# Moving 106 of 281 low-part subtractions from VectorE to GpSimd in a two-block transformer kernel

## The reference

```python
def swiglu(u, wg, wu, wd):
    return (jax.nn.silu(u @ wg) * (u @ wu)) @ wd
...
# first block, layer i: m is silu(c) @ ada_w[i] + ada_b[i], cut in 9 parts
x = x + 0.5 * m[:, 2] * swiglu(modulate(x, norm_g[i, 0], m[:, 0], m[:, 1]), ...)
x = x + m[:, 5] * mixer(...)        # layer 0: a two-way state-space scan (SSD), layer 1: pooling
x = x + 0.5 * m[:, 8] * swiglu(modulate(x, norm_g[i, 2], m[:, 6], m[:, 7]), ...)
# second block: projections (w_in_2), gated recurrence and sparse attention, w_out_2, twice
```

## Time and profile before

| | before |
|---|---|
| median of 3 runs | 2466.79 us (2463.68 to 2474.09) |
| the profiled execution | 2466.79 us, span 2465.1 us |
| PE busy | 2231.3 us (91%) |
| DVE busy | 1611.7 us (65%) |
| ACT busy | 988.4 us (40%) |
| POOL busy | 182.5 us (7%) |
| chain that ended last | PE 71%, DVE 18%, issue 6%, ACT 5% |
| low parts on VectorE, line 1631 | 281, 641.0 us |

### The profile page before, as it was taken

The page is one execution under the profiler, slowest core; times in us unless marked ns, Lnnn a source line. Parts: engine busy times, 40 slices in busy tenths (PEclk is TensorE's granted clock), DMA queues, the critical chain, the costliest instruction groups (busy, mean ns, idle before and its releaser), DMA issues.

```text
span 2465.1 us, 39886 instructions
## 1 busy us (share of the span) xinstructions
PE 2231.3 (91%) x16565; PEld 2132.5 (87%) x16565; DVE 1611.7 (65%) x2268; ACT 988.4 (40%) x1109; POOL 182.5 (7%) x152
## 2 busy tenths in 40 slices
PE   7888889988998988999899899979999999899987
PEld 6888888888985988898899899979999788799967
DVE  6877767778878976777754654456763445675453
ACT  2422254434332554332433443445444435544432
POOL 1000000000001000001000000002310000321000
PEclk7888999998998889999999999989998798899779
DMA  8565757753322426777555445534333133434301
GB/s 295 178 221 202 256 182 256 261 179 104 103 79 100 139 95 228 234 255 241 184 180 181 134 137 189 185 103 150 125 122 112 43 120 104 136 122 120 103 18 52
DMA packets 270792, 383.83 MB, mean 156 GB/s; under 512 B 8441, under 2 KB 230727, under 8 KB 270679
## 3 DMA queue, kind: packets, MB, share of 16 engines
q1 hardware_dynamic: 246983, 293.59, 36.3%
q0 software_dynamic: 22288, 85.02, 10.3%
q10 hardware_dynamic: 1408, 3.59, 0.4%
HBM read 381.06 MB, written 1.11 MB: 155 GB/s over the span
## 4 chain that ended last, share of the span: by engine, by line
PE 71%; DVE 18%; issue 6%; ACT 5%; SPq 0%; DMA 0%; DVEq 0%; ACTq 0%
PE bank L615 20%; PE bank L616 19%; PE bank L617 19%; DVE ada_acc L1677 4%; ACT w_hi L1209 3%; DVE w_lo L1631 3%; PE bank L991 2%; PE bank L628 2%; PE bank L650 1%; DVE e_long L1954 1%; DVE e_long L1972 1%; DVE rstd L1641 1%; DVE conv_acc L1903 1%; PE bank L637 1%; DVE e_short L1957 1%
## 5 line engine op out<-in xcount | busy, mean ns | idle before, releaser
L1631 DVE TENSOR_TENSOR w_lo<-raw,w_hi 128x2048 fp32r<-128x2048 f32 (+1 forms) x281 | 641.0, 2284 | 503.9 <-ACT w_hi L1209 503.6
L615 PE MATMUL bank<-u_hi,w_hi 128*128 128x256 f32 x2376 | 703.5, 296 | 26.4 <-DVE u_lo L1662 24.1
L616 PE MATMUL bank<-u_lo,w_hi 128*128 128x256 f32 x2376 | 689.4, 290 | 0.0
L617 PE MATMUL bank<-u_hi,w_lo 128*128 128x256 f32 x2376 | 688.6, 290 | 0.0
L1209 ACT ACTIVATE w_hi<-raw 128x2048 fp32r<-128x2048 f32 (+1 forms) x281 | 531.5, 1893 | 234.1 <-PE bank L617 220.3
L615 PEld LDWEIGHTS bank<-u_hi,w_hi 128*128 128x128 f32 x2376 | 472.6, 199 | 43.0 <-issue 35.0
L616 PEld LDWEIGHTS bank<-u_lo,w_hi 128*128 128x128 f32 x2376 | 474.3, 200 | 0.5 <-issue 0.5
L617 PEld LDWEIGHTS bank<-u_hi,w_lo 128*128 128x128 f32 x2376 | 473.6, 199 | 0.0
L1677 DVE SCALAR_TENSOR_TENSOR ada_acc<-ada,silu_c,ada_acc 128x256 f32<-128x256 f32 x588 | 266.5, 482 | 13.0
L615 PE MATMUL bank<-h_hi,w_hi 128*128 128x256 f32 x880 | 248.1, 282 | 20.6 <-DVE h_lo L1705 20.6
L616 PE MATMUL bank<-h_lo,w_hi 128*128 128x256 f32 x880 | 247.3, 281 | 0.0
(11 more groups left out here) (334 smaller groups left out, 3769.0 us busy)
## 6 DMA issues: line engine op xcount, KB each, us to landing
ada<-in_ada_w POOLq DMA_DIRECT2D x72, 1024.0 KB, 5.8
raw<-in_w_in SPq DMA_DIRECT2D x60, 1024.0 KB, 5.0
raw<-in_ffn_w_gate SPq DMA_DIRECT2D x55, 1024.0 KB, 7.0
raw<-in_ffn_w_up SPq DMA_DIRECT2D x55, 1024.0 KB, 5.1
raw<-in_ffn_w_down SPq DMA_DIRECT2D x55, 1024.0 KB, 5.1
raw<-in_ssd_w_in SPq DMA_DIRECT2D x20, 1024.0 KB, 5.3
raw<-in_w_out SPq DMA_DIRECT2D x16, 1024.0 KB, 5.1
raw<-in_ssd_w_out SPq DMA_DIRECT2D x8, 1024.0 KB, 5.2
```

The lines of the kernel that those rows point to most:

```text
L615: pe.matmul(out_, wh, xh, start=start, stop=False, skip_group_check=True)
L616: pe.matmul(out_, wh, xl, start=False, stop=False, skip_group_check=True)
L617: return pe.matmul(out_, wl, xh, start=False, stop=stop, skip_group_check=True)
L1631: ve.tensor_tensor(wlo[slot][:, 0:n], raw[slot][:, 0:n], whi[slot][:, 0:n].bitcast(F32), ALU.subtract)\
```

## The change

GpSimd takes over 106 of the 281 low parts: in every feed-forward the down chunks but the last (10 in each), in `ffn0` to `ffn2` also the gate chunks from block 2 on (`GATES_BY_POOL`, 9 in each), in `ffn0` also the up chunks from block 1 on (`UPS_BY_POOL`, 10), and in the state-space stage chunks 3 to 15 and 17 to 22 (19). VectorE's queue loses the same instructions. On GpSimd's queue they stand between the `ada` loads: low part of up, low part of gate, load for q+2, low part of down, load for q+3. In the state-space stage twelve stand ahead of the store of `q`, one behind the first skip product and six behind the broadcast loads of `q`. The instruction, its operands and the semaphores are the same; the engine differs.

```diff
+GATES_BY_POOL = (0, 1, 2)
+UPS_BY_POOL = (0,)
...
@@ gpsimd, in ffn(i, loads)
-                def pair(j, layer):
+                def lo(r, j):
+
+                    slot = (g + r) % SLOTS
+                    pool.wait_ge(S["hi_done"], g + r + 3 * j + 1)
+                    pool.tensor_tensor(wlo[slot][:, :], raw[slot][:, :], whi[slot][:, :].bitcast(F32), ALU.subtract)\
+                        .then_inc(lo_done[slot], 1)
+
+                def pair(j, layer, more=True, first=False):
+                    if not first and i in UPS_BY_POOL:
+                        lo(1, j)
+                    if more and not first and i in GATES_BY_POOL:
+                        lo(2, j)
                     if layer is not None:
                         load_on(0, j, layer)
+                    if more:
+                        lo(3, j)
+                    if layer is not None:
                         load_on(1, j, layer)
...
-                        pair(j0, layer)
+                        pair(j0, layer, j0 < FP - 1, j0 == 0)
...
-            ffn(0, [(1, FP - 1, 0), (FP - 1, FP, 0)])
+            ffn(0, [(0, 1, None), (1, FP - 1, 0), (FP - 1, FP, 0)])
...
@@ gpsimd, state-space stage
+            for c in range(G["ssd_in"] + 3, G["ssd_in"] + 15):
+                lo(c)
...
+                if t == 0 and h0 == 0:
+                    lo(G["ssd_in"] + 15)
...
+                if gd >= 2:
+                    lo(G["ssd_in"] + 15 + gd)
...
-            ffn(3, [(1, LAST_PAIRS, 1)])
+            ffn(3, [(0, 1, None), (1, LAST_PAIRS, 1), (LAST_PAIRS, FP - 1, None)])
+            ffn(4, [(0, 1, None), (1, FP - 1, None)])
...
@@ vector, in ffn(i)
-                    lo(g + 4, CH, j - 1)
+                    if i not in UPS_BY_POOL:
+                        lo(g + 4, CH, j - 1)
                     if vectors:
                         sum_of(q, 0, half_q, vectors)
-                    if not last:
+                    if not last and i not in GATES_BY_POOL:
                         lo(g + 5, CH, j - 1)
-                        lo(g + 6, CH, j - 1)
...
-                lo_at(g + 3)
...
@@ vector, state-space stage
-            lo_at(c0 + 3)
...
-                lo_at(c0 + 4 + i)
...
-                if 1 <= gd < 7:
-                    lo_at(c0 + 16 + gd)
```

More of the change, by code:

```diff
@@ L508, in ffn @@
             def ffn(i, loads):
+                g = G[FFNS[i][0]]
                 q0 = ADA_FIRST + ADA_FFN * i - 2
@@ L531, in _ @@
                 load_ada(q, q % 2, 0)
-            ffn(0, [(1, FP - 1, 0), (FP - 1, FP, 0)])
+            ffn(0, [(0, 1, None), (1, FP - 1, 0), (FP - 1, FP, 0)])
             second = (ADA_CHUNKS - ADA_FIRST - ADA_FFN) // 2
-            ffn(1, [(1, second, 0), (second, FP - 1, 1)])
+            ffn(1, [(0, 1, None), (1, second, 0), (second, FP - 1, 1)])
             pool.wait_ge(S["mods_done"], ADA_FIRST + 2 * ADA_FFN)
@@ L546, in _, with lo @@
                 pool.memset(cpad[i][:, :, :, :], 0.0).then_inc(S["set_up"], 1)
+            def lo(c):
+                slot = c % SLOTS
+                pool.wait_ge(S["hi_done"], c + 1)
+                pool.tensor_tensor(wlo[slot][:, :], raw[slot][:, :], whi[slot][:, :].bitcast(F32), ALU.subtract)\
+                    .then_inc(lo_done[slot], 1)
+            for c in range(G["ssd_in"] + 3, G["ssd_in"] + 15):
+                lo(c)
             pool.wait_ge(S["dt_cols"], 1)
@@ L581, in _ @@
                 .then_inc(S["pool_in"], 16)
-            ffn(2, [(1, FP - 1, 1), (FP - 1, FP, 1)])
-            ffn(3, [(1, LAST_PAIRS, 1)])
+            ffn(2, [(0, 1, None), (1, FP - 1, 1), (FP - 1, FP, 1)])
+            ffn(3, [(0, 1, None), (1, LAST_PAIRS, 1), (LAST_PAIRS, FP - 1, None)])
+            ffn(4, [(0, 1, None), (1, FP - 1, None)])
             for l in range(DEPTH):
```

## The result

The changed kernel takes 2600.99 us (median of 4 runs, 2595.12 to 2607.05), the kernel before in the same runs 2467.61 us. The ratio is 1.0535 (95% interval 1.051 to 1.0562). The forecast was slower, at 2509 us and at most 2592 us: the direction came true, the size did not.

The account below looks back on a forecast made before the run. TensorE was taken to set the end, with VectorE ahead of it in places. Terms of 21.4 + 6.3 + 3.5 + 6.5 + 4.1 = 42 us on 2466.79 gave 2509 us; 8-in-10 range 2435 to 2592 us.

Parts of the forecast that it names:

- the stall is not paid: Rival: in the 27 modulation pairs GpSimd's reads slip between VectorE's chained steps; 2379 us, chance 0.25.
- the price of one moved low part: Where VectorE always has two-input work: 3.8 us on GpSimd, stalling VectorE's queue by 3.3 us.
- B: Stall on VectorE's own queue for each low part moved to GpSimd: 3.3 us, likeliest 3.1 to 3.5.
- the price is higher: Rival: 2048 elements cost by slower GpSimd rows, stall 4.3 us or more; 2585 us; chance 0.18 together with the clock rival.
- Pairs of `ffn1` and `ffn2`: 18 one-vector pairs, gate and down moved: 21.47 us against 20.28, +1.19 us each, +21.4 us.
- Pairs of `ffn0`: All three low parts moved: six two-vector pairs +6.3 us, three one-vector pairs +3.5 us.
- State-space stage: Six scan low parts +6.5 us, four early convolution ones +4.1 us, the other moved ones zero.
- as long as B is under 4.0 us: Later state-space convolutions: VectorE's 1.75 us wait for ScalarE hides the 1.03 us loss, zero below that stall.
- +1.03 each: First four convolution low parts, VectorE back to back: stall replaces a 2.27 us low part, +4.1 us together.
- The scan's term: Six scan low parts amid gapless two-input VectorE work: +(3.3 - 2.21) x 6 = +6.5 us.
- `ffn3` and `ffn4`, GpSimd's queue, the loads: 20 down low parts covered by TensorE's 12 us; loads and stores delayed behind low parts still timely: all zero.
- TensorE's clock: Rival: added TensorE waits lower its clock, 2.2 us in each of 27 pairs; 2569 us; chance 0.18 together with higher price.

Follow-up runs that it names:

- write-only kernel: Changed kernel with state-space low parts back on VectorE and GpSimd's feed-forward low parts replaced by a one-column subtraction and two memsets: 2388.34 us, ratio 0.9683.
- experiment 4: Changed kernel with all 106 GpSimd low parts reading `raw` twice, 3.60 us in place of 4.56, `w_lo` zero: 2512.17 us, ratio 1.0166.
- experiment 6: Changed kernel with both `ada` loads of a pair issued behind the down low part on GpSimd: 2681.8 us, ratio 1.0857.

## Why the prediction was right and wrong

**Right: the mechanism.** VectorE and GpSimd keep each other out of SBUF, whole instructions at a time, as the earlier trace rows had it. The write-only kernel shows that neither GpSimd's writes nor its busy time hold up the chained steps. The Trainium skill (SBUF — State Buffer, section Who interferes with whom) says that a VectorE instruction with two SBUF inputs contends with a GpSimd instruction that reads SBUF, and not with one that only writes it. The stalls of 4.20 us and the steps of 482 ns beside memsets agree. What the forecast did not have is that "turns" are not strict: in the scan one of GpSimd's low parts stood behind nearly 8 us of VectorE's instructions, and in the write-only kernel a VectorE step stood behind two memsets. The rival "the stall is not paid" is out. Its price was a fair one: 2401 us without the state-space gain, and the write-only kernel takes 2388.

**Wrong: the step "the price of one moved low part".** It took 3.8 us for the instruction and 3.3 us for B, and held to the level differences "because they have the same two plain inputs". They don't: one is a broadcast, and so is one input of the multiplication in the earlier trace rows from which the 3.1 us came. The instruction takes 4.56 us and B is 4.20 and 5.03 us in a pair of `ffn1`, 4.6 us on average. How much each place lost follows. The rival "the price is higher" (B of 4.3 or more, 2585 us and above) is what happened, and the figure of the Trainium skill that the forecast set aside, by which the sum would have been near 2590 us, was the better one.

**Pairs of `ffn1` and `ffn2`: forecast +21.4, measured +54.1 us.** With 9.23 us for the two stalls in place of 6.6 the term is 24.10 - 20.28 = 3.8 us, times 18, or 69 us. That is too much by 15, from a second slip in the same step: 20.28 us was the length of the fastest pairs. The six pairs of `ffn1` from 398.19 to 524.19 in the earlier trace rows are 126.00 us, 21.0 each, because two of them ran at a lower clock. From 21.0 the sum is 3.1 x 18 = 56 us, within 2 us of the measurement. With this base and the forecast's B it would have been +8 us. So it is partly luck that the short version of experiment 4, whose low parts are about as long as the forecast had them, lands at 2512 us beside the forecast 2509. Its `ffn0` is +10.4 us (forecast 9.8), its `ffn1` +8.1 (10.7), its state-space stage +16.0 (10.6).

**Pairs of `ffn0`: forecast +9.8, measured +32.4.** The three pairs with one vector went from 62.0 to 74.2 us, +12.2, forecast +3.5. The six with two vectors went from 149.9 to 172.8 us, +22.9, forecast +6.3. They were to take 16.32 + 3B, with the measured stalls over 29 us. The first takes 32.6 us, the others 28.0 on average. The timeline of one of 27.6 us shows why:

```profile
156.90 5.62 DVE L1709 SCALAR_TENSOR_TENSOR ada_acc<-ada,silu_c,ada_acc 128x256 f32<-128x256 f32 x14
166.64 0.17 DVE L1719 TENSOR_TENSOR mods<-bank,cols 128x8 f32 x1 [4.12 <-PE bank L682]
...
142.86 9.35 POOL L525 TENSOR_TENSOR w_lo<-raw,w_hi 128x2048 fp32r<-128x2048 f32 x2 [3.13 <-ACT w_hi L1241]
...
158.04 8.92 POOL L525 TENSOR_TENSOR w_lo<-raw,w_hi 128x2048 fp32r<-128x2048 f32 x1
```

Up and gate low part stretch sum q from 6.15 to 14.6 us (141.87 to 156.46), by 8.4. The down low part comes at 158.04, in sum q+1, whose steps keep their usual 5.62 us; it is GpSimd that waits, until VectorE is done at 162.52, and it ends 4.4 us later. VectorE is not stalled a third time. But its wait for `ada_sums` of q+1, which TensorE comes to only behind the up chunk, holds it 4.12 us, and from the end of the sum to the end of `h_lo` it is 6.77 us in place of 4.02. 16.32 + 8.4 + 2.75 = 27.5 us. So here it is two stalls and a wait for TensorE, where the forecast had three stalls.

**State-space stage: forecast +10.6, measured +34.7.** By the starts of the `conv`s, it divides as follows. Up to the first one, the low part in the dt chain: +0.4, forecast zero. From the first to the fifth: 33.34 to 46.32 us, +13.0, forecast +4.1. From the fifth to the twelfth: 90.59 to 99.19 us, +8.6, forecast zero "as long as B is under 4.0 us". From there to VectorE's first wait for `cb` in the scan: 52.51 to 56.52 us, +4.0, forecast zero. The scan with its six low parts (777.39 to 884.39 before, 863.35 to 976.24 after): 107.00 to 112.89 us, +5.9, forecast +6.5. The rest: +2.9, forecast zero.

In the first four of the convolution, the step "+1.03 each" set a stall against the low part that went and forgot that this low part had filled a time in which VectorE would else wait for ScalarE. For the later ones B is above the 4.0 us that was named as the end of the cover, but only by 0.2 us each, and they lost 1.2 on average. VectorE still waits 0.8 to 3.6 us for `conv_pad` in each of the last ones, so ScalarE runs later too: its own wait for `conv_acc` went from 39.6 to 73.4 us. Which of ScalarE's operations makes it late was not followed up.

The scan's term came out nearly as forecast, but not by its working. VectorE waits there 2.13 us for `cb` in every second step, and every second low part gets in during that wait:

```profile
886.64 2.54 DVE L2001 SCALAR_TENSOR_TENSOR e_long<-e_long,tok_cols,cb 128x256 f32<-128x256 f32 x1 [2.13 <-ACT cb L1445]
...
890.43 4.72 DVE L2003 SCALAR_TENSOR_TENSOR e_short<-e_short,tok_cols,cb 128x128 f32<-128x128 f32 x1
```

Three low parts stall VectorE 2.1 us (2.54 in place of 0.48), the three that follow them 4.2 to 4.4 us (4.72 in place of 0.34). That is 19.2 us, less six times 2.21, or 6.0 us: a B of 3.2 us on average, from another cause than the forecast's 3.3.

**`ffn3` and `ffn4`, GpSimd's queue, the loads: forecast nothing, and nearly nothing it was.** `ffn4` has -0.4 us, and the write-only kernel, with the same queue, lost nothing. `ffn3` has +2.5 us, and about as much in every kernel with full low parts there (210.2 to 211.6 us against 208.5).

**The second block, +9.7 us, with no changed line.** In the other kernels' profiles the same code takes 843.8 to 853.6 us, against 843.8 in the profile of before. It is thus within the spread of single profiles, from the low end of it to the high. The rival "TensorE's clock" is seen only in part: `ffn1` went from 0.96 to 0.93, `ffn2` from 0.94 to 0.89, and TensorE's busy time in `ffn2` from 215.78 to 228.11 us. It comes with the waits, and no run takes the two apart.

## What to carry to other kernels

Before work moves to an idle engine, price the moved instruction by a row with the same operand forms (dense, broadcast, one tensor or two), and ask for how long it will keep the other engine out of memory; here 2.2 us of VectorE became 4.2 to 5.0 us of VectorE. If the reason for the move is a wait in an in-order queue, try first to put other ready work ahead of the waiting instruction: that alone gave 3.7%, with nothing moved. And place a stall by who is behind it: with the same two low parts a pair took 24.1 us when they were spread and 27.6 when they stood together ahead of TensorE's reduction.

## What the runs showed of the hardware

- GpSimd's `tensor_tensor` of 128x2048: 4.56 us with two different dense inputs, 3.60 us with a broadcast input or the same tensor twice, 4.70 us with float32 in place of fp32r output; 2.39 us for 1024.
- A memset of 128x3072 (2.66 us) or 128x2047 (1.81 us) on GpSimd stalls no VectorE step with two wide inputs: the slowest of 588 is 490 ns. It does stall a TENSOR_SCALAR of 128x256 with one wide input: 27 of 84 took over 0.6 us, up to 4.63, in place of 0.35.
- Low parts keep that TENSOR_SCALAR out as well: 3.69 us in place of 0.35. It is a short form, 0.35 us where a SCALAR_TENSOR_TENSOR of the same size takes 0.48; whether all one-input instructions behave so no run shows.
- The waiting goes the other way too. In the scan one of GpSimd's low parts took 12.23 us:

```profile
916.56 0.34 DVE L1986 SCALAR_TENSOR_TENSOR e_short<-q_bcast,tok_cols,consts 128x128 f32<-128x128 f32 x1
919.03 2.61 DVE L2001 SCALAR_TENSOR_TENSOR e_long<-e_long,tok_cols,cb 128x256 f32<-128x256 f32 x1 [2.13 <-ACT cb L1445]
...
909.13 12.23 POOL L569 TENSOR_TENSOR w_lo<-raw,w_hi 128x2048 fp32r<-128x2048 f32 x1 [4.58 <-ACT w_hi L1241]
```

It ended at 921.36, 4.46 us after VectorE's first gap began at 916.90; until then VectorE ran unhindered. In the pair of `ffn1` shown, where each step of `ada_acc` waits for the one before, GpSimd's low part of 458.45 keeps out the step that starts 0.27 us later. With two vectors a step waits only for the one before of its own vector, so the steps follow each other more closely (14 in 5.62 us against 7 in 3.61). There it got in at once at 142.86 and only at the end of the sum at 158.04. What decides it is open.
- The down low part in `ffn1` starts right behind the issue of an `ada` load (0.90 us), and VectorE's stall is 5.03 us, 0.8 us more than without one. In the changed kernel 21 low parts right behind an issue stall a step of `ada_acc` by 4.74 to 5.20 us, and each of these steps had started 0.35 to 0.79 us ahead of the low part. Those with no issue ahead stall one by 4.14 to 4.38 us. An issue alone stalls nothing (experiment 6). A step is 0.48 us long by itself, so by these records the hold begins while the issue still runs, but only where a low part is queued right behind it. Start times on GpSimd are rough in the profile, and why it is so is open.
